# Two products of a feed-forward chunk in one 512-column matmul, with the halves added on VectorE

## The chip, the core and the metric

The kernel runs on one core of a Trainium2 chip. The metric is device time in microseconds of one execution, as a median over runs. The profile is of one such execution.

## The reference

The network works on one sequence of 256 tokens with 1024 channels, in float32. It has attention, recurrent and memory blocks, and six feed-forward blocks. The change touches only the latter:

```python
def squared_relu_mlp(h, w1, w2):          # twice, FF_DIM = 4096
    a = jax.nn.relu(h @ w1)
    return (a * a) @ w2

def swiglu(x, w_in, w_out):               # four times, D_FF = 2816
    gate, up = jnp.split(x @ w_in, 2, axis=-1)
    return (jax.nn.silu(gate) * up) @ w_out
```

## The kernel before

Weights stream from HBM in chunks of 1 MB (128x2048 float32), one after another through a ring of three slots. The queue SP loads a chunk into `raw`. ScalarE rounds it to fp32r in `w_hi` (`hi`, L628). VectorE subtracts, `raw - w_hi`, and has the rest in `w_lo` (`lo`, L1021). Activations are kept in the same two parts: `at_h` and `at_l` (or `mem_h` and `mem_l`), 8 k-tiles of 128 rows and 256 tokens, and `hid_h`, `hid_l` for the hidden layer. A product of two such pairs is three fp32r matmuls: high by high, high by low, low by high.

A column chunk (`col_chunk`, L1580) makes 256 hidden columns: two halves `i` of 128, in each 8 k-tiles `k`, in each the three products with 256 moving columns (the tokens), so 48 matmuls into one PSUM bank of `C`. In these chunks the weights are stationary. A row chunk (`row_chunk`, L1593) multiplies 256 hidden columns by their 1024 output columns in 24 matmuls of 512 columns, into the four banks of `Y`.

In a feed-forward block all engines follow an order written out by hand, in hardware loops (`Fori`):

- The squared-ReLU block (`relu_ff`) has 16 steps. TensorE does `up(j + 1)`, one column chunk, and then `down(j)`, the row chunk of the step before. Its hidden values come from ScalarE (`units`: Relu out of `C`, L753, Square into `full`, L755, Square into `hid_h`, L756) and VectorE (`units`: `hid_l`, L1155).
- The SwiGLU block (`swiglu`) has 11 steps. TensorE does the gate chunk and the up chunk of step `j + 1` (`gate_up`) and then `down(j)`. ScalarE takes the Silu of the gate chunk out of `C` (L788). VectorE multiplies it by the up chunk, twice (L1184 and L1185), and subtracts (L1187).
- The first chunks of a block (`front_part`, L1535) hold the activations stationary, so that work can start before the second block of tokens is normalised. Their result is transposed back (`front_turn`) into `C[:, 0, :]`.

Each instruction waits for its data on a semaphore: `chunk_done` counts finished chunks, `hid_lo` says that a step's hidden values are there, `lo_split` that a chunk's `w_lo` is. A load into a slot of `raw` waits for the `lo` of the chunk three before; a `hi` waits for the matmuls of the chunk three before. An engine takes its instructions in order, so what stands behind a wait waits too. Names such as `relu`, `full`, `pr` and `total` are parts of one buffer, which the profile calls arena.

Of the kernel before, what the change touches and what calls it, by code (L numbers as in the profile page):

```python
# [14 lines left out]
P = 128  # L15
# [26 lines left out]
class Counts:  # L42


    def __init__(self, norm, rms, xn, turned, x, y, chunk, copied, hid, hid_hi, up, head, ctx, rot, front):
        self.norm, self.rms, self.xn, self.turned, self.x, self.y = norm, rms, xn, turned, x, y
        self.chunk, self.copied = chunk, copied
        self.hid, self.hid_hi, self.up, self.head, self.ctx, self.rot, self.front = hid, hid_hi, up, head, ctx, rot, front

# [58 lines left out]
def build(nc, a, out):  # L108
# [15 lines left out]
    with ctx:  # L124
# [5 lines left out]
        xn = sb("xn", [P, TB, D])  # L130
        at_h = sb("at_h", [P, KT, S], f32r)
        at_l = sb("at_l", [P, KT, S], f32r)
        mem_h = sb("mem_h", [P, KT, S], f32r)
        mem_l = sb("mem_l", [P, KT, S], f32r)
        hid_h = sb("hid_h", [P, 3, 2 * S], f32r)
# [79 lines left out]
        full = pr  # L215


# [14 lines left out]
        first_gain_in = sem("first_gain_in")  # L232
        gains_in = [sem(f"gains_in{i}") for i in range(2)]
        front_ready, front_turned, front_hi = sem("front_ready"), sem("front_turned"), sem("front_hi")
        hid_hi = sem("hid_hi")
# [137 lines left out]
        def counts(s):  # L373

            if s[0] == "norm":
                return dict(norm=1, rms=s[1] != "same", xn=2, turned=4 * (s[1] != "out"))
            if s[0] == "post":
                return dict(norm=1, rms=1, x=2)
            if s[0] == "meanwhile":
                return dict(norm=2, rms=2, x=2, xn=2, turned=4, chunk=len(s[1]), copied=len(s[1]))  # L380
            if s[0] == "add":
                return dict(x=2)
            if s[0] == "cols":
                return dict(chunk=len(s[1]), copied=len(s[1]))
            if s[0] == "even_cols":
                return dict(norm=1, rms=1, xn=2, turned=4, chunk=len(s[1]), copied=len(s[1]))
            if s[0] == "rows":
                return dict(chunk=4, y=1)
            if s[0] == "relu_ff":
                return dict(chunk=2 * N_REL, y=1, copied=N_REL, hid=N_REL, hid_hi=N_REL, front=1)  # L390
            if s[0] == "swiglu":
                return dict(chunk=3 * N_GLU, y=1, copied=N_GLU, up=N_GLU - 1, hid=N_GLU, front=1)
# [12 lines left out]
        before, so_far = [], dict(norm=0, rms=0, xn=0, turned=0, x=0, y=0, chunk=0, copied=0, hid=0,  # L405
                                  hid_hi=0, up=0, head=0, ctx=0, rot=0, front=0)
        for s in net:
# [14 lines left out]
        def behind_post(at):  # L422

            return Counts(at.norm + 1, at.rms + 1, at.xn, at.turned, at.x + 2, at.y, at.chunk, at.copied, at.hid,
                          at.hid_hi, at.up, at.head, at.ctx, at.rot, at.front)

# [180 lines left out]
        def _(act):  # L607
# [132 lines left out]
            def front_out(at):  # L740

                act.wait_ge(front_turned, at.front + 1)
                return nc.scalar.activation(hid_h[:, 0, :], C[:, 0, :], ACT.Copy)

            def relu_ff(at, same):
                n = at.chunk

                def units(j, t=None):


                    step = (lambda v: v) if t is None else (lambda v: t * 3 + v)
                    act.wait_ge(chunk_done, n + 2 * j if t is None else t * 6 + (n + 2 * j))
                    nc.scalar.activation(relu[j % 3], C[:, j % 3, :], ACT.Relu).then_inc(cols_copied, 1)  # L753
                    act.wait_ge(cols_copied, step(at.copied + j + 1))
                    nc.scalar.activation(full[j % 3], relu[j % 3], ACT.Square)  # L755
                    nc.scalar.activation(hid_h[:, j % 3, :], relu[j % 3], ACT.Square).then_inc(hid_hi, 1)  # L756
# [15 lines left out]

                with nc.scalar.Fori(0, REL_TURNS) as t:
                    for j in range(1, 4):
                        two(j, t)
# [230 lines left out]
        def _(dve):  # L1006
# [137 lines left out]
            def front_out(at, turned_hi, count):  # L1144

                dve.wait_ge(turned_hi, count)
                V.tensor_tensor(hid_l[:, 0, :], C[:, 0, :], hid_h[:, 0, :].bitcast(f32), ALU.subtract).then_inc(hid_lo, 1)

            def relu_ff(at):
                n = at.chunk  # L1150

                def units(j, t=None):

                    dve.wait_ge(hid_hi, at.hid_hi + j + 1 if t is None else t * 3 + (at.hid_hi + j + 1))
                    V.tensor_tensor(hid_l[:, j % 3, :], full[j % 3], hid_h[:, j % 3, :].bitcast(f32),  # L1155
                                    ALU.subtract).then_inc(hid_lo, 1)
# [11 lines left out]

                with nc.vector.Fori(0, REL_TURNS) as t:
                    for j in range(1, 4):  # L1170
                        two(j, t)
# [344 lines left out]
        def _(pe):  # L1516
# [29 lines left out]
            def front_turn(at):  # L1546

                pe.wait_ge(front_ready, at.front + 1)
                for b in range(TB):
                    for k in range(2):  # L1550
                        last = nc.tensor.transpose(C[:, 0, k * S + b * P:k * S + (b + 1) * P],
                                                   full[0][:, b * S + k * P:b * S + (k + 1) * P], ident[:])
                last.then_inc(front_turned, 1)

            def col_chunk(n, kind, h, l, bank, t=None, split=None, some=range(2)):
# [103 lines left out]
            def relu_ff(at, same):  # L1659
                n = at.chunk  # L1660

                def up(j, t=None):

                    col_chunk(n + 2 * j - 1, "T", at_h, at_l, C[:, j % 3, :], t)

# [6 lines left out]
                front_one(n, front_bank(same), at, Y if same else C)  # L1672
                col_chunk(n + 1, "T", at_h, at_l, C[:, 1, :], some=[0])
                front_turn(at)
                col_chunk(n + 1, "T", at_h, at_l, C[:, 1, :], some=[1])
                down(0)
                with nc.tensor.Fori(0, REL_TURNS) as t:
                    for j in range(1, 4):
                        up(j + 1, t)
# [6 lines left out]
            def swiglu(at, same):  # L1686
                n = at.chunk
                h, l = (mem_h, mem_l) if same else (at_h, at_l)

                def gate_up(j, t=None):  # L1690
# [17 lines left out]
                front_part(n + 1, h, l, 1, Y[:, 1, :], split).then_inc(chunk_done, 1)  # L1708
                col_chunk(n + 2, "T", h, l, C[:, 2, :])
                front_turn(at)  # L1710
                col_chunk(n + 3, "T", h, l, C[:, 3, :])
                if at.rot > 0:
# [351 lines left out]
```

## Time and profile before

| | |
|---|---|
| median of 3 runs | 1869.29 us (1868.24 to 1869.43) |
| the profiled execution, its own time | 1868.2 us |
| its span, first to last instruction | 1866.2 us |
| mean granted TensorE clock | 0.995 of 2.4 GHz |
| busy: TensorE, VectorE, ScalarE | 97%, 55%, 46% of the span |

Between the end of the span and the time of the execution lie 2.0 us. The busy time of matmuls counts the overlap of one with the next, so the distance between the starts of neighbours is what one costs, not its own duration.

### The profile page before, as it was taken

Reading aid. Unit: us, or ns where it says so; the run is one execution under the profiler, and the core shown is the slowest. Engines: PE = TensorE matmul, PEld = TensorE weight load, DVE = VectorE, ACT = ScalarE, POOL = GpSimd, SP = SyncE. Lnnn points to the kernel's source line nnn. Section 1 sums busy time; section 2 is a strip of 40 time slices with the busy share of each in tenths; the row PEclk is TensorE's granted clock in tenths of the full one; section 3 lists DMA queues with packets and bytes.
Section 4 is the critical chain, followed back from the end, with each engine's and each line's share of the span. In section 5 each row is a group of like instructions: output and inputs, shape, how many; then the busy total and the mean of one; then the engine's idle time right before and its main releaser. Section 6 shows DMA issues by size and latency. Waiting matters only on the chain.

```text
span 1866.2 us, 29807 instructions
## 1 busy us (share of the span) xinstructions
PE 1814.5 (97%) x12635; PEld 1666.3 (89%) x12635; DVE 1020.6 (55%) x1037; ACT 857.0 (46%) x1044; POOL 71.0 (4%) x117
## 2 busy tenths in 40 slices
PE   7999999999999999999999999999999999899998
PEld 6989989998988989998999898899989998779997
DVE  5666465446566464446554554645565555765554
ACT  5535454446455454555333455533344334454333
POOL 1000000000120000000000011000000000110000
PEclk9999999999999999999999999999999999999999
DMA  8607446565546356554555544555555554336552
GB/s 270 218 23 226 136 159 189 193 189 180 175 153 203 112 169 194 190 190 162 189 180 181 169 129 149 178 181 185 191 168 195 187 180 158 113 114 204 180 181 89
DMA packets 224440, 318.69 MB, mean 171 GB/s; under 512 B 5569, under 2 KB 194129, under 8 KB 224353
## 3 DMA queue, kind: packets, MB, share of 16 engines
q1 hardware_dynamic: 219552, 301.48, 49.3%
q0 software_dynamic: 4800, 15.94, 2.7%
q8 instruction: 67, 1.10, 0.2%
q14 instruction: 21, 0.16, 0.0%
HBM read 316.35 MB, written 1.05 MB: 170 GB/s over the span
## 4 chain that ended last, share of the span: by engine, by line
PE 92%; DVE 4%; ACT 1%; DMA 1%; issue 1%; POOL 0%; SPq 0%; DVEq 0%; ACTq 0%
PE C L1580 45%; PE Y L1593 29%; PE Y L1580 7%; PE Y L1535 3%; DVE w_lo L1021 1%; DVE xn L1050 1%; DMA raw<-in_w_in_ab 1%; PE C L1982 1%; PE C L1829 1%; PE C L1737 1%; PE Y L1961 1%; PE C L1776 1%; PE Y L1784 1%; PE C L1638 1%; PE Y L1754 0%
## 5 line engine op out<-in xcount | busy, mean ns | idle before, releaser
L1021 DVE TENSOR_TENSOR w_lo<-raw,w_hi 128x2048 fp32r<-128x2048 f32 x284 | 650.2, 2290 | 486.0 <-ACT w_hi L628 485.7
L628 ACT ACTIVATE w_hi<-raw 128x2048 fp32r<-128x2048 f32 x284 | 542.4, 1910 | 361.0 <-PE Y L1593 219.8
L1580 PE MATMUL C<-at_h,w_hi 128*128 128x256 f32 x1664 | 465.2, 284 | 0.3 <-DVE at_l L1064 0.3
L1580 PE MATMUL C<-at_l,w_hi 128*128 128x256 f32 x1664 | 464.1, 283 | 0.7 <-DVE at_l L1064 0.7
L1580 PE MATMUL C<-at_h,w_lo 128*128 128x256 f32 x1664 | 464.0, 283 | 0.0
L1580 PEld LDWEIGHTS C<-at_l,w_hi 128*128 128x128 f32 x1664 | 316.2, 192 | 3.6 <-DVE at_l L1064 0.9
L1580 PEld LDWEIGHTS C<-at_h,w_hi 128*128 128x128 f32 x1664 | 316.1, 192 | 3.2 <-issue 1.0
L1580 PEld LDWEIGHTS C<-at_h,w_lo 128*128 128x128 f32 x1664 | 316.1, 192 | 0.0
L1593 PE MATMUL Y<-w_hi,hid_h 128*128 128x512 f32 x656 | 204.4, 393 | 3.5 <-issue 3.5
L1593 PE MATMUL Y<-w_lo,hid_h 128*128 128x512 f32 x656 | 203.0, 390 | 0.0
L1593 PE MATMUL Y<-w_hi,hid_l 128*128 128x512 f32 x656 | 202.7, 390 | 0.0
L1593 PEld LDWEIGHTS Y<-w_lo,hid_h 128*128 128x128 f32 x656 | 123.5, 188 | 26.6
L1593 PEld LDWEIGHTS Y<-w_hi,hid_l 128*128 128x128 f32 x656 | 123.4, 188 | 26.2
L1593 PEld LDWEIGHTS Y<-w_hi,hid_h 128*128 128x128 f32 x656 | 118.7, 189 | 24.4 <-issue 4.3
L1580 PE MATMUL C<-mem_h,w_hi 128*128 128x256 f32 x448 | 126.8, 283 | 0.0
L1580 PE MATMUL C<-mem_h,w_lo 128*128 128x256 f32 x448 | 126.8, 283 | 0.0
L1580 PE MATMUL C<-mem_l,w_hi 128*128 128x256 f32 x448 | 126.8, 283 | 0.0
L788 ACT ACTIVATE arena<-C 128x512 f32<-128x512 f32 x40 | 23.9, 597 | 153.0 <-PE C L1580 153.0
L1580 PEld LDWEIGHTS C<-mem_l,w_hi 128*128 128x128 f32 x448 | 86.0, 192 | 0.5
L1580 PEld LDWEIGHTS C<-mem_h,w_hi 128*128 128x128 f32 x448 | 86.0, 192 | 0.5
L1580 PEld LDWEIGHTS C<-mem_h,w_lo 128*128 128x128 f32 x448 | 86.0, 192 | 0.0
L1580 PE MATMUL Y<-at_h,w_hi 128*128 128x256 f32 x272 | 77.9, 286 | 0.0
(277 smaller groups left out, 2377.8 us busy)
## 6 DMA issues: line engine op xcount, KB each, us to landing
raw<-in_ffn_w_in SPq DMA_DIRECT2D x88, 1024.0 KB, 5.1
raw<-in_w_ff SPq DMA_DIRECT2D x64, 1024.0 KB, 5.3
raw<-in_ffn_w_out SPq DMA_DIRECT2D x44, 1024.0 KB, 4.9
raw<-in_w_mem_kv SPq DMA_DIRECT2D x16, 1024.0 KB, 5.3
raw<-in_w_qkv SPq DMA_DIRECT2D x12, 1024.0 KB, 5.1
raw<-in_sb_w_qkv SPq DMA_DIRECT2D x12, 1024.0 KB, 5.1
raw<-in_w_in_ab SPq DMA_DIRECT2D x10, 1024.0 KB, 8.0
raw<-in_w_mem_q SPq DMA_DIRECT2D x8, 1024.0 KB, 5.5
```

Source lines behind the costliest of these rows:

```text
L628: nc.scalar.activation(w_hi[:, n % RING, :], raw[:, n % RAW, :], ACT.Copy).then_inc(hi_split, 1)
L788: nc.scalar.activation(relu[j % 2], C[:, 2 * (j % 2), :], ACT.Silu).then_inc(cols_copied, 1)
L1021: V.tensor_tensor(w_lo[:, n % RING, :], raw[:, n % RAW, :], w_hi[:, n % RING, :].bitcast(f32), ALU.subtract).then_inc(lo_split, 1)
L1050: return V.scalar_tensor_tensor(xn[:, b, :], src, stat[:, 6, j:j + 1], gain[:, at.norm % 2, :], ALU.mult, ALU.mult)
L1535: last = mm(to[:, b * S:(b + 1) * S], still[:, k, part], moving[:, k, :], start=j == 0 and k == 0, stop=j == 2 and k == KT - 1)
L1580: last = mm(to, *passes[k][j], start=step == 0, stop=step == 3 * KT - 1)
L1593: last = mm(Y[:, 2 * b + half, :], still[:, part], moving[:, k, half * 512:(half + 1) * 512], start=first and k == 0 and j == 0, stop=end ...
L1638: last = nc.tensor.transpose(banks[:, 2 * b + h, k * P:(k + 1) * P], xn[:, b, (4 * h + k) * P:(4 * h + k + 1) * P], ident[:])
L1737: last = mm(C[:, i % 2, b * S:(b + 1) * S], qT[:, 2 * i + k, b * P:(b + 1) * P], mem_kT[:, 2 * i + k, :], start=k == 0, stop=k == 1)
L1776: last = nc.tensor.transpose(C[:, 2 + h % 2, k * P:(k + 1) * P], pair_pr[p % 3][:, h % 2, k * P:(k + 1) * P], ident[:])
L1784: last = mm(to[64 * (h % 2):64 * (h % 2) + 64, kb * P:S], vt[:, kb, value(h) * 64:value(h) * 64 + 64], head_pT[h % 4][:, kb * S:S + kb * P ...
L1829: mm(to[:, 0:SEEN], suffix_c, keep, start=False, stop=False, skip_group_check=True)
```

## The change

`at_h` and `at_l` become two halves of one tensor `at_hl` (and likewise `mem_hl`), so that for each k-tile the 256 high and the 256 low columns lie side by side. In the feed-forward loops `pair_chunk` takes the place of `col_chunk`. For each k-tile it issues one 512-column matmul, whose left half is `w_hi` by high and whose right half is `w_hi` by low, and one 256-column matmul, `w_lo` by high, which is added to the right half. A chunk then fills two banks of `C` in place of one, and the hidden columns are the sum of the two halves of each bank. VectorE makes this sum with `reduce_sum` over 128x1024 values in PSUM, into `total` in SBUF, whence ScalarE and VectorE go on. In `swiglu` the gate chunk now always has banks 0 and 1 and the up chunk banks 2 and 3, so TensorE waits for the sum of the step before (`gate_summed`, `up_summed`) ahead of writing them. `front_turn` goes to `Y[:, 2, :]`. The loops of `relu_ff` do six steps in a turn in place of three.

```diff
+        at_hl = sb("at_hl", [P, KT, 2, S], f32r)
+        mem_hl = sb("mem_hl", [P, KT, 2, S], f32r)
+        at_h, at_l, mem_h, mem_l = (t[:, :, i, :] for t in (at_hl, mem_hl) for i in range(2))
...
+        total = pT
...
+        def halves_of(pair):
+
+            return C[:, 2 * pair:2 * pair + 2, :].rearrange("p i (a n) -> p i n a", a=2)
...
@@ ScalarE, relu_ff units
-                    act.wait_ge(chunk_done, n + 2 * j if t is None else t * 6 + (n + 2 * j))
-                    nc.scalar.activation(relu[j % 3], C[:, j % 3, :], ACT.Relu).then_inc(cols_copied, 1)
+                    act.wait_ge(up_summed, step(at.summed + j))
+                    nc.scalar.activation(relu[j % 3], total[j % 3], ACT.Relu).then_inc(cols_copied, 1)
@@ ScalarE, swiglu gate
-                    act.wait_ge(chunk_done, step(6, n + 3 * j))
-                    nc.scalar.activation(relu[j % 2], C[:, 2 * (j % 2), :], ACT.Silu).then_inc(cols_copied, 1)
+                    act.wait_ge(gate_summed, step(2, at.up + j))
+                    nc.scalar.activation(relu[j % 2], total[0], ACT.Silu).then_inc(cols_copied, 1)
@@ VectorE, relu_ff units
+                    dve.wait_ge(chunk_done, n + 2 * j if t is None else t * 6 + (n + 2 * j))
+                    V.reduce_sum(tiles(total[j % 3], 2), halves_of(j % 2), X).then_inc(up_summed, 1)
                     dve.wait_ge(hid_hi, at.hid_hi + j + 1 if t is None else t * 3 + (at.hid_hi + j + 1))
@@ VectorE, swiglu units
                     dve.wait_ge(chunk_done, step(6, n + 3 * j + 1))
+                    V.reduce_sum(tiles(total[1], 2), halves_of(1), X).then_inc(up_summed, 1)
                     dve.wait_ge(cols_copied, step(2, at.copied + j + 1))
-                    up = C[:, 2 * (j % 2) + 1, :]
+                    dve.wait_ge(up_summed, step(2, at.summed + j))
+                    up = total[1]
@@ VectorE, swiglu
+                def gate(j, t=None):
+
+                    step = (lambda k, v: v) if t is None else (lambda k, v: t * k + v)
+                    dve.wait_ge(chunk_done, step(6, n + 3 * j))
+                    if j >= 2:
+                        dve.wait_ge(cols_copied, step(2, at.copied + j))
+                    V.reduce_sum(tiles(total[0], 2), halves_of(0), X).then_inc(gate_summed, 1)
+
                 def three(j, t=None):
                     b = n + 2 + 3 * j + AHEAD
                     lo(b, t)
+                    gate(j + 1, t)
@@ TensorE
-                        last = nc.tensor.transpose(C[:, 0, k * S + b * P:k * S + (b + 1) * P],
+                        last = nc.tensor.transpose(Y[:, 2, k * S + b * P:k * S + (b + 1) * P],
...
+            def pair_chunk(n, hl, pair, t=None, some=range(2)):
...
+                for i in some:
+                    part = slice(i * P, (i + 1) * P)
+                    to = C[:, 2 * pair + i, :]
+                    for k in range(KT):
+                        mm(tiles(to, 2), wh[:, k, part], hl[:, k, :, :], start=k == 0, stop=False)
+                        last = mm(to[:, S:2 * S], wl[:, k, part], hl[:, k, 0, :], start=False, stop=k == KT - 1)
...
@@ TensorE, relu_ff
-                    col_chunk(n + 2 * j - 1, "T", at_h, at_l, C[:, j % 3, :], t)
+                    pair_chunk(n + 2 * j - 1, at_hl, j % 2, t)
...
-                with nc.tensor.Fori(0, REL_TURNS) as t:
-                    for j in range(1, 4):
+                with nc.tensor.Fori(0, REL_TURNS, 2) as t:
+                    for j in range(1, 7):
@@ TensorE, swiglu
-                    col_chunk(n + 3 * j - 1, "T", h, l, C[:, 2 * (j % 2), :], t)
-                    col_chunk(n + 3 * j, "T", h, l, C[:, 2 * (j % 2) + 1, :], t)
+                    if j >= 2:
+                        pe.wait_ge(gate_summed, at.up + j - 1 if t is None else t * 2 + (at.up + j - 1))
+                    pair_chunk(n + 3 * j - 1, hl, 0, t)
+                    if j >= 2:
+                        pe.wait_ge(up_summed, at.summed + j - 1 if t is None else t * 2 + (at.summed + j - 1))
+                    pair_chunk(n + 3 * j, hl, 1, t)
```

What stands in order on two engines shows the change in the instructions. On TensorE, the first matmuls of the loop of the squared-ReLU block, before:

```order
L1677 ISA
L1580 MATMUL C<-at_h,w_hi 128x256
L1580 MATMUL C<-at_l,w_hi 128x256
L1580 MATMUL C<-at_h,w_lo 128x256
L1580 MATMUL C<-at_h,w_hi 128x256
L1580 MATMUL C<-at_l,w_hi 128x256
L1580 MATMUL C<-at_h,w_lo 128x256
```

The same place on TensorE after the change:

```order
L1708 ISA
L1581 MATMUL C<-at_hl,w_hi 128x512
L1582 MATMUL C<-at_hl,w_lo 128x256
L1581 MATMUL C<-at_hl,w_hi 128x512
L1582 MATMUL C<-at_hl,w_lo 128x256
L1581 MATMUL C<-at_hl,w_hi 128x512
```

Where there were three matmuls of 256 columns for a k-tile, there are one of 512 and one of 256, and these two lengths alternate.

On VectorE, one step of the loop of the SwiGLU block, before (rows of register arithmetic stand between the instructions):

```order
L1021 TENSOR_TENSOR w_lo<-raw,w_hi 128x2048
L1020 REGISTER_ALU
L1021 TENSOR_TENSOR w_lo<-raw,w_hi 128x2048
L1182 REGISTER_ALU
L1184 TENSOR_TENSOR arena<-C,arena 128x512
L1185 TENSOR_TENSOR hid_h<-C,arena 128x512
L1186 REGISTER_ALU
L1187 TENSOR_TENSOR hid_l<-arena,hid_h 128x512
L1020 REGISTER_ALU
L1021 TENSOR_TENSOR w_lo<-raw,w_hi 128x2048
```

The same step on VectorE after the change:

```order
L1025 TENSOR_TENSOR w_lo<-raw,w_hi 128x2048
L1210 TENSOR_REDUCE arena<-C 128x512
L1024 REGISTER_ALU
L1025 TENSOR_TENSOR w_lo<-raw,w_hi 128x2048
L1188 TENSOR_REDUCE arena<-C 128x512
L1189 REGISTER_ALU
L1190 REGISTER_ALU
L1192 TENSOR_TENSOR arena<-arena 128x512
L1193 TENSOR_TENSOR hid_h<-arena 128x512
L1194 REGISTER_ALU
L1195 TENSOR_TENSOR hid_l<-arena,hid_h 128x512
```

The sum of the gate chunk now stands between the first two `lo` of a step, and that of the up chunk ahead of the three elementwise operations, whose operands are all in SBUF.

## Rows read from the trace of the kernel before

**Rows 1.** The page: busy time by engine, and the chain that ended last by line.

```profile
PE 1814.5 (97%) x12635; PEld 1666.3 (89%) x12635; DVE 1020.6 (55%) x1037; ACT 857.0 (46%) x1044; POOL 71.0 (4%) x117
...
PE C L1580 45%; PE Y L1593 29%; PE Y L1580 7%; PE Y L1535 3%; DVE w_lo L1021 1%; DVE xn L1050 1%; DMA raw<-in_w_in_ab 1%; PE C L1982 1%; PE C L1829 1%; PE C L1737 1%; PE Y L1961 1%; PE C L1776 1%; PE Y L1784 1%; PE C L1638 1%; PE Y L1754 0%
```

**Rows 2.** Windows view: busy time by engine in most of a SwiGLU block.

```profile
895.63:1053.90 158.27, 158.27 (x1105) 148.47 (x1105) 80.20 (x55) 60.70 (x42) 0.00 (x0) 1.00 0.56 186
```

**Rows 3.** Chain in order of time (start us, us, what): last steps of two blocks.

```profile
429.69 5.47 PE Y L1593 x24
435.15 5.75 PE C L1580 x48
440.91 8.20 PE Y L1593 x36
...
1031.47 11.51 PE C L1580 x96
1042.98 10.92 PE Y L1593 x48
```

**Rows 4.** Timeline, TensorE and its weight loads (start us, us): row chunk to column chunk.

```profile
333.56 0.62 PE L1593 MATMUL Y<-w_hi,hid_l 128*128 128x512 f32 x2
334.01 0.28 PE L1580 MATMUL C<-at_h,w_hi 128*128 128x256 f32 x1
...
335.09 0.28 PE L1580 MATMUL C<-at_h,w_hi 128*128 128x256 f32 x1
...
333.79 0.19 PEld L1580 LDWEIGHTS C<-at_h,w_hi 128*128 128x128 f32 x1
```

**Rows 5.** Timeline, TensorE, 850 to 871 us: 512-column fp32r and bf16, 128-column transposes.

```profile
850.99 0.62 PE L1593 MATMUL Y<-w_hi,hid_l 128*128 128x512 f32 x2
...
856.43 0.62 PE L1593 MATMUL Y<-w_hi,hid_l 128*128 128x512 f32 x2
...
858.25 4.71 PE L1654 MATMUL C<-zeros 128*128 128x512 bf16 x21
...
870.46 1.03 PE L1638 MATMUL C<-ident,xn 128*128 128x128 f32 x8
```

**Rows 6.** Timeline, TensorE: the first 512-column matmuls behind 256-column ones.

```profile
328.55 0.63 PE L1593 MATMUL Y<-w_hi,hid_h 128*128 128x512 f32 x2
329.01 0.62 PE L1593 MATMUL Y<-w_lo,hid_h 128*128 128x512 f32 x2
329.48 0.62 PE L1593 MATMUL Y<-w_hi,hid_l 128*128 128x512 f32 x2
```

**Rows 7.** Groups of instructions by form, VectorE (count, busy us, mean ns, idle before).

```profile
L1137 DVE SCALAR_TENSOR_TENSOR x<-Y,x 128x1024 f32<-128x1024 f32 x12 | 14.7, 1225 | 27.4 <-PE Y L1593 27.4
L1235 DVE TENSOR_REDUCE arena<-C 128x2 f32<-128x512 f32 x8 | 5.5, 692 | 11.6 <-PE C L1737 11.6
L1389 DVE RECIPROCAL arena<-arena 128x512 f32<-128x512 f32 x1 | 3.3, 3345 | 0.0
```

**Rows 8.** Timeline, ScalarE and VectorE: the hidden values of a squared-ReLU block's last step.

```profile
440.95 0.60 ACT L753 ACTIVATE arena<-C 128x512 f32<-128x512 f32 x1 [3.78 <-PE C L1580]
...
442.76 0.69 DVE L1155 TENSOR_TENSOR hid_l<-arena,hid_h 128x512 fp32r<-128x512 f32 x1 [3.27 <-ACT hid_h L756]
```

**Rows 9.** Timeline, ScalarE and VectorE: the last step of a SwiGLU block.

```profile
1037.26 0.60 ACT L788 ACTIVATE arena<-C 128x512 f32<-128x512 f32 x1 [3.78 <-PE C L1580]
...
1039.69 2.29 DVE L1021 TENSOR_TENSOR w_lo<-raw,w_hi 128x2048 fp32r<-128x2048 f32 x1 [3.88 <-ACT w_hi L628]
1043.02 0.69 DVE L1184 TENSOR_TENSOR arena<-C,arena 128x512 f32<-128x512 f32 x1 [1.04 <-PE C L1580]
...
1044.34 0.69 DVE L1187 TENSOR_TENSOR hid_l<-arena,hid_h 128x512 fp32r<-128x512 f32 x1
```

**Rows 10.** Waits (us, times, longest), and page: a DMA issue (KB, us to landing).

```profile
ACT w_hi L628 <- DMA raw<-in_w_in_ab: 7.5, 1, 7.5
...
raw<-in_ffn_w_in SPq DMA_DIRECT2D x88, 1024.0 KB, 5.1
```

More of the change, by code:

```diff
@@ L42, with __init__ @@
 class Counts:
-    def __init__(self, norm, rms, xn, turned, x, y, chunk, copied, hid, hid_hi, up, head, ctx, rot, front):
+    def __init__(self, norm, rms, xn, turned, x, y, chunk, copied, hid, hid_hi, up, head, ctx, rot, front, summed):
         self.norm, self.rms, self.xn, self.turned, self.x, self.y = norm, rms, xn, turned, x, y
         self.chunk, self.copied = chunk, copied
-        self.hid, self.hid_hi, self.up, self.head, self.ctx, self.rot, self.front = hid, hid_hi, up, head, ctx, rot, front
+        self.hid, self.hid_hi, self.up, self.head, self.ctx, self.rot, self.front, self.summed = hid, hid_hi, up, head, ctx, rot, front, summed
 def constants():
@@ L130, in build @@
         xn = sb("xn", [P, TB, D])
[L131 to L134, printed above, removed]
+        at_hl = sb("at_hl", [P, KT, 2, S], f32r)
+        mem_hl = sb("mem_hl", [P, KT, 2, S], f32r)
+        at_h, at_l, mem_h, mem_l = (t[:, :, i, :] for t in (at_hl, mem_hl) for i in range(2))
         hid_h = sb("hid_h", [P, 3, 2 * S], f32r)
@@ L233, in build @@
         gains_in = [sem(f"gains_in{i}") for i in range(2)]
+        gate_summed, up_summed = sem("gate_summed"), sem("up_summed")
         front_ready, front_turned, front_hi = sem("front_ready"), sem("front_turned"), sem("front_hi")
@@ L389, in counts @@
             if s[0] == "relu_ff":
-                return dict(chunk=2 * N_REL, y=1, copied=N_REL, hid=N_REL, hid_hi=N_REL, front=1)
+                return dict(chunk=2 * N_REL, y=1, copied=N_REL, hid=N_REL, hid_hi=N_REL, front=1, summed=N_REL - 1)
             if s[0] == "swiglu":
-                return dict(chunk=3 * N_GLU, y=1, copied=N_GLU, up=N_GLU - 1, hid=N_GLU, front=1)
+                return dict(chunk=3 * N_GLU, y=1, copied=N_GLU, up=N_GLU - 1, hid=N_GLU, front=1, summed=N_GLU - 1)
             if s[0] == "softmax":
@@ L405, in build @@
         before, so_far = [], dict(norm=0, rms=0, xn=0, turned=0, x=0, y=0, chunk=0, copied=0, hid=0,
-                                  hid_hi=0, up=0, head=0, ctx=0, rot=0, front=0)
+                                  hid_hi=0, up=0, head=0, ctx=0, rot=0, front=0, summed=0)
         for s in net:
@@ L424, in behind_post @@
             return Counts(at.norm + 1, at.rms + 1, at.xn, at.turned, at.x + 2, at.y, at.chunk, at.copied, at.hid,
-                          at.hid_hi, at.up, at.head, at.ctx, at.rot, at.front)
+                          at.hid_hi, at.up, at.head, at.ctx, at.rot, at.front, at.summed)
         SEEN_BLOCKS = ((0, P), (P, SEEN))
@@ L742, in front_out @@
                 act.wait_ge(front_turned, at.front + 1)
-                return nc.scalar.activation(hid_h[:, 0, :], C[:, 0, :], ACT.Copy)
+                return nc.scalar.activation(hid_h[:, 0, :], Y[:, 2, :], ACT.Copy)
             def relu_ff(at, same):
@@ L771, in two @@
                     hi(n + 2 + 2 * j + AHEAD, t)
-                with nc.scalar.Fori(0, REL_TURNS) as t:
-                    for j in range(1, 4):
+                with nc.scalar.Fori(0, REL_TURNS, 2) as t:
+                    for j in range(1, 7):
                         two(j, t)
@@ L1146, in front_out @@
                 dve.wait_ge(turned_hi, count)
-                V.tensor_tensor(hid_l[:, 0, :], C[:, 0, :], hid_h[:, 0, :].bitcast(f32), ALU.subtract).then_inc(hid_lo, 1)
+                V.tensor_tensor(hid_l[:, 0, :], Y[:, 2, :], hid_h[:, 0, :].bitcast(f32), ALU.subtract).then_inc(hid_lo, 1)
             def relu_ff(at):
@@ L1167, in two @@
                     lo(n + 2 + 2 * j + AHEAD, t)
-                with nc.vector.Fori(0, REL_TURNS) as t:
-                    for j in range(1, 4):
+                with nc.vector.Fori(0, REL_TURNS, 2) as t:
+                    for j in range(1, 7):
                         two(j, t)
@@ L1550, in front_turn @@
                     for k in range(2):
-                        last = nc.tensor.transpose(C[:, 0, k * S + b * P:k * S + (b + 1) * P],
+                        last = nc.tensor.transpose(Y[:, 2, k * S + b * P:k * S + (b + 1) * P],
                                                    full[0][:, b * S + k * P:b * S + (k + 1) * P], ident[:])
                 last.then_inc(front_turned, 1)
+            def pair_chunk(n, hl, pair, t=None, some=range(2)):
+                split_ready(n, t)
+                wh, wl = (w[:, n % RING, :].rearrange("p (k c) -> p k c", k=KT) for w in (w_hi, w_lo))
+                for i in some:
[4 more added lines that the diff above has]
+                        last = mm(to[:, S:2 * S], wl[:, k, part], hl[:, k, 0, :], start=False, stop=k == KT - 1)
+                if 1 in some:
+                    last.then_inc(chunk_done, 1)
             def col_chunk(n, kind, h, l, bank, t=None, split=None, some=range(2)):
@@ L1672, in relu_ff @@
                 front_one(n, front_bank(same), at, Y if same else C)
-                col_chunk(n + 1, "T", at_h, at_l, C[:, 1, :], some=[0])
+                pair_chunk(n + 1, at_hl, 1, some=[0])
                 front_turn(at)
-                col_chunk(n + 1, "T", at_h, at_l, C[:, 1, :], some=[1])
+                pair_chunk(n + 1, at_hl, 1, some=[1])
                 down(0)
-                with nc.tensor.Fori(0, REL_TURNS) as t:
-                    for j in range(1, 4):
+                with nc.tensor.Fori(0, REL_TURNS, 2) as t:
+                    for j in range(1, 7):
                         up(j + 1, t)
@@ L1688, in swiglu @@
                 h, l = (mem_h, mem_l) if same else (at_h, at_l)
+                hl = mem_hl if same else at_hl
                 def gate_up(j, t=None):
-                    col_chunk(n + 3 * j - 1, "T", h, l, C[:, 2 * (j % 2), :], t)
-                    col_chunk(n + 3 * j, "T", h, l, C[:, 2 * (j % 2) + 1, :], t)
+                    if j >= 2:
[4 more added lines that the diff above has]
+                    pair_chunk(n + 3 * j, hl, 1, t)
                 def down(j, t=None, end=False):
@@ L1708, in swiglu @@
                 front_part(n + 1, h, l, 1, Y[:, 1, :], split).then_inc(chunk_done, 1)
-                col_chunk(n + 2, "T", h, l, C[:, 2, :])
+                pair_chunk(n + 2, hl, 0)
                 front_turn(at)
-                col_chunk(n + 3, "T", h, l, C[:, 3, :])
+                pair_chunk(n + 3, hl, 1)
                 if at.rot > 0:
```

## The prediction, made before the changed kernel was run

> **What bounds the kernel now.** I read the busy shares of the page first, then the chain that ended last, and then, since a share of busy time says nothing of a single stage, the chain in order of time and a window over one SwiGLU block. TensorE is busy 97% of the span and the next engine 55%, and 45% of the span lies on the chain as column chunks of line 1580 [rows 1]. In the window TensorE is busy 158.27 of 158.27 us and VectorE 80.20 [rows 2]. In the chain the chunks stand end to end: the row chunk at 429.69, the column chunk at 435.15 and the next row chunk at 440.91 leave no gap; neither do 1031.47 and 1042.98 [rows 3]. So in the feed-forward loops nothing but the rate at which TensorE starts matmuls sets the time, and whatever is added on VectorE is free until it makes TensorE wait.
>
> **What a matmul costs.** From the first 256-column matmul at 334.01 to the one at 335.09 there are nine starts, 1.08 / 9 = 120 ns each [rows 4]. For 512 columns, 24 starts lie between 850.99 and 856.43, 5.44 / 24 = 226.7 ns [rows 5]. The columns themselves stream in 256 / 2.4 = 106.7 ns and 512 / 2.4 = 213.3 ns at the granted clock of 1.00 in the window [rows 2]. Each matmul therefore carries 13.3 ns beyond its columns, and the same at both lengths. That is the term on which the forecast rests: one instruction less saves one such charge, while the number of streamed columns, 768 per k-tile, stays.
>
> **The change, part by part.**
>
> *Matmuls.* Per k-tile it was 3 x 120 = 360 ns and becomes 226.7 + 120 = 346.7 ns, so 13.3 ns less. Both lengths have been measured only among their own kind, save at the seams of chunks. There, a 256-column matmul follows a 512-column one without loss: the last pair of 512 starts at 333.56 and the 256 at 334.01, which is 225 ns each [rows 4]. The load of its weights starts at 333.79, with the matmul before it, so it has that matmul's stream as cover. The changed chunks are 15 for each of the two squared-ReLU blocks and 20 for each of the four SwiGLU blocks (the first chunk, or the first two, are made by the front part and stay). That is 30 + 80 = 110 chunks with 16 k-tiles each, 1760 in all. 1760 x 13.3 ns = 23.4 us.
>
> The bounds of this price: at worst the seam in the other direction recurs. The first 512-column matmuls behind 256-column ones start at 328.55, 329.01 and 329.48 in pairs, 0.93 / 4 = 232 ns each, and up to 235 in the second pair [rows 6]. Then a k-tile costs 235 + 120 = 355 and the change saves 5 x 1760 = 8.8 us. At best the 256-column matmul, with its load hidden behind a long one, falls toward the 128-column transposes' distance, (1.03 - 0.27) / 7 = 109 ns, where 0.27 is about what the last one's own duration adds [rows 5]. A k-tile is then 336 and the saving 24 x 1760 = 42 us. I take 13.3, since the charge is equal at two lengths and the seam loss fades within a few matmuls.
>
> The Trainium skill, on the page "TensorE: Matmul & The Clock Gate", section "Back-to-back issue gap", puts the distance of warm matmuls at N / 2.4 plus 2.5 ns. By that the merge would save 2.5 x 1760 = 4.4 us only. The trace has a row that agrees, the bf16 matmuls at 858.25 (21 in 4.71 us, so (4.71 - 0.40) / 20 = 216 ns), but the fp32r rows, which are those of this change, do not [rows 5].
>
> *Sums on VectorE.* 110 reductions of 1024 columns out of PSUM are added. The trace has none of this form. The nearest rows are a 1024-column operation out of PSUM at 1225 ns and a reduction over 512 columns at 692 ns [rows 7]; both say about 1.2 us. The lower bound is 0.69 us, if only the 512 results counted. The upper one, at the rate of the slowest row (3345 ns for 512), is 6.7 us. I take 1.23 us, as both nearer rows give one column per step. What hides them: per SwiGLU step VectorE has three `lo` of 2.29 us and 2.0 us of elementwise work [rows 9], 8.9 us, and with 2.5 us of sums 11.4, against a step of 16.98 us that shrinks to 16.55. In a squared-ReLU step it has 2 x 2.29 + 0.69 + 1.23 = 6.5 us, and stands about 1.8 us more in the wait for ScalarE, against 11.0 us.
>
> *The longer chain to the hidden values.* In the loops a row chunk comes a whole chunk or two after the column chunk it needs, and the chain is tight only at a block's end. In the squared-ReLU block the last column chunk ends at 440.91, the values are ready at 443.45 [rows 3, 8], and the second to last row chunk covers until 440.91 + 5.47 = 446.38. A sum of 1.23 us and a handshake of some 0.05 put them at 444.7, 1.6 us to spare. Behind the sum on VectorE wait `hid_l` and the next `lo`; it slides from 444.6 to 445.9, and the chunk it makes is of the following stage, more than 5 us later. In the SwiGLU block the Silu at 1037.26 slides by 1.3 us, with it the `hi` behind it and the `lo` that began at 1039.69, which ends at 1043.3 in place of 1041.98 [rows 9]. That is 0.3 us after the up chunk is done at 1042.98. The sum ends at 1044.5, and `hid_l` at about 1046.5, where the cover goes to 1048.45 [rows 3]. Again 1.9 us to spare, so I price it at nothing. With the cover gone each microsecond of delay costs one at six block ends.
>
> *Banks and loads.* The new waits of TensorE on `gate_summed` come after an up chunk and a row chunk, 11 us behind the gate chunk; the sum is there after 1.3. No load is late: in the whole trace ScalarE's `hi` waited once for a DMA, at the start [rows 10]. A `lo` that slides by 1.3 to 1.6 us moves its slot's load, which lands 5.1 us after issue [rows 10], while the slot is wanted only when the chunk after next is done, some 9 us or more behind that `lo`. ScalarE and VectorE reading `total` in SBUF in place of PSUM, the front's transpose into `Y`, and the longer loop body cost nothing that I can place: TensorE showed no gap at any turn of a loop [rows 3].
>
> **The sum.** 1868.2 - 23.4 = 1844.8 us for an execution such as the profiled one. The median of the runs lies 1.1 us above the profiled execution, so I expect 1845.9 as a median, say 1846.
>
> **The rivals.**
>
> *Alternating lengths keep the seam's loss.* For it speaks that the only 512-column matmuls seen right behind 256-column ones are slower (232 to 235 ns) [rows 6]. Against it: they lose as a group of six or so, also where they follow each other, and the change has equally many seams back. It gives 1868.2 - 8.8 = 1859.4, as a median 1860.5. Chance 0.12.
>
> *The charge is not per matmul.* If what a merge saves is only what the bf16 row shows beyond its columns, 216 - 213.3 = 2.7 ns, it is 4.8 us, and the median 1864.5. Against it stand the equal 13.3 ns at two lengths. The page's rule named above would give the same within 0.4 us. Chance 0.05.
>
> *More is saved,* as the load of a long matmul's weights or the pair's shared bank costs less than a charge each: up to 42 us, 1827. Chance 0.06.
>
> *The sum is slow, and VectorE becomes the bound.* The place is the SwiGLU step: 8.9 us plus two sums fill 16.98 us once a sum takes 4.0 us; from there on the kernel is slower, for the gain is gone and each further 0.1 us costs 36 x 0.2 = 7 us. At 6.7 us a sum, the step takes 22.3 us, 5.3 more in 36 steps, so 190 us more, some 2060 before the squared-ReLU blocks are counted. For it speaks only that the reduction reads two values 256 columns apart, a form no row shows. Against it, the reduction row [rows 7]. Chance 0.04.
>
> **How the numbers follow.** The forecast itself has 0.73; its own range, with the load and handshake terms a few microseconds off, is 1841 to 1852. The range of 8 in 10 takes in the seam rival: 1840 to 1861. A change of under 0.2% (3.7 us) can't be told from none here. Faster by more: 0.73 + 0.12 + 0.06, and nearly all of the 0.05, since 4.8 us is just over, so 0.94. Same: 0.02. Slower: 0.04.
>
> **What would show it.** In the changed profile the chain should have 32 matmuls of a column chunk in 16 x 346.7 = 5.55 us in place of 5.75 (x48), steps of 11.01 and 16.56 us, still without gaps; VectorE's reduction at about 1.23 us; the second to last and the last row chunk of each block still end to end. A start distance of 512-column matmuls in these chunks above 232 ns would be the seam rival; a wait of TensorE for `hid_l` or for a sum would prove my slack wrong; a reduction above 3 us would turn the sign into a question.

## The result, and the profile after

The changed kernel takes 1857.18 us as a median of 4 runs (1855.62 to 1857.87), against 1869.36 us before (1868.24 to 1870.82, 4 runs). The ratio is 0.9939, with a 95% interval of 0.9926 to 0.9952. It is faster, by 12.2 us, about half of the 23.4 us that were forecast. The profiled execution took 1857.76 us, its span is 1856.0 us.

The first rows are of the changed kernel's page: busy time by engine, the chain that ended last by line, and the costliest group of each of the new lines (the form, count, busy us, mean ns). The line numbers are those of the changed kernel: 1581 is the 512-column matmul of `pair_chunk`, 1582 the 256-column one, 1624 the row chunk, 1611 `col_chunk`.

```profile
PE 1806.5 (97%) x10875; PEld 1574.8 (85%) x10875; DVE 1151.2 (62%) x1147; ACT 859.4 (46%) x1044; POOL 71.0 (4%) x117
...
PE Y L1624 29%; PE C L1581 22%; PE C L1582 11%; PE C L1611 11%; PE Y L1611 7%; PE Y L1552 3%; DVE w_lo L1025 1%; DVE xn L1054 1%; PE C L2018 1%; DMA raw<-in_w_in_ab 1%; PE C L1865 1%; PE C L1773 1%; PE C L1812 1%; PE Y L1997 1%; PE C L1669 1%
...
L1581 PE MATMUL C<-at_hl,w_hi 128*128 128x512 f32 x1440 | 511.3, 399 | 0.0
L1582 PE MATMUL C<-at_hl,w_lo 128*128 128x256 f32 x1440 | 405.0, 281 | 0.0
...
L1210 DVE TENSOR_REDUCE arena<-C 128x512 f32<-128x1024 f32 x40 | 49.0, 1225 | 55.7 <-PE C L1582 55.7
```

The 45% of column chunks on the chain [rows 1] are now 22 + 11 + 11, the last of them in chunks that the change leaves alone. The sum of the gate chunk took 1225 ns, the other two 1218 and 1224, and VectorE's share rose from 55 to 62%. Both new matmul groups show no idle time before them. The windows view of a SwiGLU block, which answers to [rows 2], says so too: TensorE is busy all of it.

```profile
895.63:1048.00 152.37, 152.37 (x794) 129.79 (x794) 99.88 (x73) 58.46 (x38) 0.00 (x0) 1.00 0.56 189
```

So no wait has come in. The steps are nevertheless too long. In the chain in order of time (start us, us, what) the row chunks of neighbouring steps lie 11.11 us apart in a squared-ReLU block (5.640 for the column chunk and 5.467 for the row chunk) and 16.79 us in a SwiGLU block (11.290 and 5.504). Before it was 11.22 and 16.98 [rows 3]; 11.01 and 16.56 were forecast.

```profile
294.96 5.46 PE Y L1624 x24
306.06 5.46 PE Y L1624 x24
...
987.37 5.50 PE Y L1624 x24
1004.16 5.50 PE Y L1624 x24
```

Where the time goes is seen in the timeline of TensorE (start us, us):

```profile
948.68 0.40 PE L1581 MATMUL C<-at_hl,w_hi 128*128 128x512 f32 x1
948.91 0.28 PE L1582 MATMUL C<-at_hl,w_lo 128*128 128x256 f32 x1
949.02 0.40 PE L1581 MATMUL C<-at_hl,w_hi 128*128 128x512 f32 x1
949.26 0.28 PE L1582 MATMUL C<-at_hl,w_lo 128*128 128x256 f32 x1
949.38 0.40 PE L1581 MATMUL C<-at_hl,w_hi 128*128 128x512 f32 x1
949.62 0.28 PE L1582 MATMUL C<-at_hl,w_lo 128*128 128x256 f32 x1
949.74 0.40 PE L1581 MATMUL C<-at_hl,w_hi 128*128 128x512 f32 x1
```

From 948.68 to 949.74 there are three pairs in 1.06 us, 353.3 ns each, where 346.7 had been forecast and three matmuls of 256 columns took 360. The pattern repeats after three pairs: the long one is followed after 233, 241 and 236 ns, the short one after 117, 120 and 113.

For the comparisons below, one number was taken from every trace: the six feed-forward blocks, each from the first transpose of `front_turn` to the start of its last row-chunk matmul. It leaves out the rest of the network, which no kernel here changes and which differed by up to 6 us between executions (840.6 to 846.8 us). The sum is 1020.9 us before and 1010.3 us after, 10.5 us less.

### The profile page after: what moved, and what is told of

Read it like the earlier page. It is cut to its first block, busy times and chain, and to the rows that moved or that the text cites. A ratio compares the mean times of both kernels' runs of the same rounds, so it can differ in the third digit from the quotient of the medians.

```text
span 1856.0 us, 26531 instructions
## 1 busy us (share of the span) xinstructions
PE 1806.5 (97%) x10875; PEld 1574.8 (85%) x10875; DVE 1151.2 (62%) x1147; ACT 859.4 (46%) x1044; POOL 71.0 (4%) x117
## 4 chain that ended last, share of the span: by engine, by line
PE 93%; DVE 4%; ACT 2%; DMA 1%; issue 1%; POOL 0%; SPq 0%; DVEq 0%; ACTq 0%
PE Y L1624 29%; PE C L1581 22%; PE C L1582 11%; PE C L1611 11%; PE Y L1611 7%; PE Y L1552 3%; DVE w_lo L1025 1%; DVE xn L1054 1%; PE C L2018 1%; DMA raw<-in_w_in_ab 1%; PE C L1865 1%; PE C L1773 1%; PE C L1812 1%; PE Y L1997 1%; PE C L1669 1%
## 5 line engine op out<-in xcount | busy, mean ns | idle before, releaser
L1581 PE MATMUL C<-at_hl,w_hi 128*128 128x512 f32 x1440 | 511.3, 399 | 0.0
L1582 PE MATMUL C<-at_hl,w_lo 128*128 128x256 f32 x1440 | 405.0, 281 | 0.0
L1581 PEld LDWEIGHTS C<-at_hl,w_hi 128*128 128x128 f32 x1440 | 271.0, 188 | 65.6
L1582 PEld LDWEIGHTS C<-at_hl,w_lo 128*128 128x128 f32 x1440 | 272.5, 189 | 2.1
L1581 PE MATMUL C<-mem_hl,w_hi 128*128 128x512 f32 x320 | 113.5, 399 | 0.0
L1611 PE MATMUL Y<-at_hl,w_hi 128*128 128x256 f32 x544 | 99.3, 285 | 0.0
L1582 PE MATMUL C<-mem_hl,w_lo 128*128 128x256 f32 x320 | 90.0, 281 | 0.0
L1611 PEld LDWEIGHTS Y<-at_hl,w_hi 128*128 128x128 f32 x544 | 84.7, 192 | 0.5 <-ACT arena L710 0.3
L1210 DVE TENSOR_REDUCE arena<-C 128x512 f32<-128x1024 f32 x40 | 49.0, 1225 | 55.7 <-PE C L1582 55.7
L1624 PE MATMUL Y<-w_hi,at_hl 128*128 128x512 f32 x288 | 79.6, 393 | 1.8 <-DVE at_hl L1486 1.6
L1611 PE MATMUL C<-at_hl,w_hi 128*128 128x256 f32 x448 | 77.4, 286 | 1.0 <-DVE at_hl L1068 1.0
```

The lines of the kernel that those rows point to most:

```text
L1210: V.reduce_sum(tiles(total[0], 2), halves_of(0), X).then_inc(gate_summed, 1)
L1581: mm(tiles(to, 2), wh[:, k, part], hl[:, k, :, :], start=k == 0, stop=False)
L1582: last = mm(to[:, S:2 * S], wl[:, k, part], hl[:, k, 0, :], start=False, stop=k == KT - 1)
L1611: last = mm(to, *passes[k][j], start=step == 0, stop=step == 3 * KT - 1)
L1624: last = mm(Y[:, 2 * b + half, :], still[:, part], moving[:, k, half * 512:(half + 1) * 512], start=first and k == 0 and j == 0, stop=end ...
```

## The experiments

The theory was that 512-column fp32r matmuls are slow behind shorter ones, whatever else the core does. The rivals were that the sums on VectorE or their waits take the missing 11 us, and that it is the operands: writing twice to the same half of a bank, or the load of new weights.

**TensorE alone, fifteen streams.** A kernel in which TensorE runs 48 matmuls or pairs of each kind, with nothing on the other engines. For the alternating streams:

```diff
+ for i in range(n):
+     mm(C[:, 2, :], W(2 * i), H(i, 512), start=i == 0, stop=False)
+     mm(C[:, 2, 256:512], W(2 * i + 1), H(i, 256), start=False, stop=i == n - 1)
```

> This kernel leaves the network out: TensorE alone runs fifteen streams of 48 matmuls or pairs, one after another, each from a source line of its own, and the output is zeros. Read is the mean distance of starts in each stream. All theories: 256 columns alone 120 ns, 512 alone 227 ns. Theory of lengths (a change of length between neighbours costs time, whatever the operands): fp32r pairs of 512 and 256 cost 353 ns in all of the same bank, another bank and the same weights; two and two falls to about 350 per pair, eight and eight to 347 to 348; 384 columns alone 173.3 ns, so 346.7 for two. Theory of the shared bank (adding to the half that the matmul before has just written costs time): 353 ns in the same bank, 347 in the other bank, and grouping changes nothing. Theory of weight loads (the load of new fp32r weights doesn't fit behind 256 columns): with the same kind of load 353, in bf16 pairs the sum of the two single distances.

Distances, from the starts in the trace, once a stream repeats (per matmul, or per pair of a long and a short one):

| stream | measured | columns / 2.4 + 13.3 ns each |
|---|---|---|
| 256 alone; 384 alone; 512 alone | 120.0; 173.3; 226.7 ns | 120.0; 173.3; 226.7 |
| 512 and 256 in turn, same bank | 353.3 | 346.7 |
| the same, 256 into another bank | 353.3 | 346.7 |
| the same, both with the same weights | 353.3 | 346.7 |
| two of 512, two of 256 | 348.3 | 346.7 |
| eight of 512, eight of 256 | 349.2 | 346.7 |
| 384 and 256 in turn | 293.3 | 293.3 |
| 128 alone; 512 and 128 in turn | 111.7; 340.0 | 66.7; 293.3 |
| bf16: 256 alone; 512 alone; in turn | 109.2; 215.8; 325.0 | |
| 512 in fp32r, 256 in bf16, in turn | 358.3 | |

The rows of three of them in the timeline: two and two, 384 alone, and bf16 in turn.

```profile
92.80 8.52 PE L97 MATMUL C<-h,w 128*128 128x384 f32 x48
...
101.86 0.62 PE L102 MATMUL C<-h,w 128*128 128x512 f32 x2
102.32 0.40 PE L104 MATMUL C<-h,w 128*128 128x256 f32 x2
...
103.95 0.63 PE L102 MATMUL C<-h,w 128*128 128x512 f32 x2
...
167.19 0.38 PE L128 MATMUL C<-hb,wb 128*128 128x512 bf16 x1
167.41 0.27 PE L129 MATMUL C<-hb,wb 128*128 128x256 bf16 x1
167.51 0.38 PE L128 MATMUL C<-hb,wb 128*128 128x512 bf16 x1
```

48 matmuls of 384 columns take from 92.80 to the next stream at 101.16, 174 ns each (the first seven distances are longer, then it is 173.3). Two and two cost 103.95 - 101.86 = 2.09 us for six pairs, 348.3 ns. In bf16 a pair costs 0.32 us, the sum of its parts. The whole loss of the changed kernel, 6.7 ns a pair, is there with VectorE and ScalarE idle; it is not a matter of the bank. Equal weights change nothing either, but they are loaded again each time. The bf16 pairs lose nothing, as the theory of weight loads expected, so the load is not ruled out. And 384 with 256 has no loss, so it isn't any change of length.

**TensorE alone, lengths and groups.** Eighteen further streams.

> The network is left out again: TensorE alone runs eighteen streams of fp32r matmuls, and the output is zeros. If any change of length costs, the pairs 512 and 384, 512 and 320, 512 and 224, 512 and 192, 480 and 256, 448 and 256, 448 and 320, 384 and 192 all lie some 7 ns above the sum of their columns at 2.4 GHz plus 26.7. The first streams have 384 and 256 at no loss, so the theory that only a matmul longer than some length is slow behind a shorter one expects a loss for 512 and perhaps 480 and 448, and none for 384 and 192. Groups of 3, 4, 6 and 16: if the loss is 26 ns for the first six long ones behind short ones less 7 given back, a pair costs 346.7 + 20 / g, so 351.7 at 4, 350 at 6 and 347.9 at 16; but two and two was at 348.3 where this gives 356.7, so it may instead be flat near 349 and fall only beyond 8. Moving columns from another buffer for the short one: 353.3 as in the kernel, if addresses play no part.

| stream | measured | columns / 2.4 + 13.3 for each matmul | loss |
|---|---|---|---|
| 512 and 384 | 413.3 ns | 400.0 | 13.3 |
| 512 and 320 | 380.0 | 373.3 | 6.7 |
| 512 and 224 | 343.3 | 333.3 | 10.0 |
| 512 and 192 | 344.4 | 320.0 | 24.4 |
| 480 and 256 | 333.3 | 333.3 | 0 |
| 448 and 256; 448 and 320 | 320.0; 346.7 | 320.0; 346.7 | 0 |
| 384 and 192 | 290.0 | 266.7 | 23.3 |
| 512 and 256 from another buffer | 353.3 | 346.7 | 6.7 |
| groups of 3; 4; 6; 16 | 350.0; 350.8; 350.0; 347.9 | 346.7 | 3.3; 4.2; 3.3; 1.3 |
| 512, 256, 256 in turn | 466.7 | 466.7 | 0 |
| 512, 512, 256 in turn | 586.7 | 573.3 | 13.3 |
| 320; 448; 480 alone | 146.7; 202.7; 216.7 | 146.7; 200.0; 213.3 | 0; 2.7; 3.3 |

```profile
99.08 0.38 PE L96 MATMUL C<-h,w 128*128 128x480 f32 x1
...
99.75 0.38 PE L96 MATMUL C<-h,w 128*128 128x480 f32 x1
99.96 0.28 PE L97 MATMUL C<-h,w 128*128 128x256 f32 x1
...
100.41 0.38 PE L96 MATMUL C<-h,w 128*128 128x480 f32 x1
```

These are four pairs of 480 and 256 in 100.41 - 99.08 = 1.33 us. With a short one of 224 to 384 columns, the pair loses time only with the full 512, and 480 with 256 has no loss. Two things limit this reading. The column for comparison is not the sum of the two single streams everywhere: 480 and 448 alone cost 16.7 and 16.0 ns beyond their columns and not 13.3, so their pairs with 256 are even some 3 ns faster than that sum. And a long matmul behind a short one doesn't lose as such: with two short ones behind each long one (512, 256, 256) the three cost just their price.

The losses with 192 and 128 columns are probably another matter. The stream of 128 columns alone has a load of weights every 111.7 ns, where the columns stream in 53.3, and in the pairs with 128, 192 and 224 columns two loads stand 108 ns apart at the closest. So the load may be what is late behind so short a matmul; no run here separates the two. The expectation that groups of 3 and 4 would cost 353 and 352 was wrong; groups lose 1.7 ns a pair at two, 3.3 to 4.2 at three to six, 2.5 at eight and 1.3 at sixteen.

**480 columns in the network.** The same test inside the kernel; left out is the product of the high weights with the low activations of the last 32 tokens, in seven of eight k-tiles.

```diff
-                        mm(tiles(to, 2), wh[:, k, part], hl[:, k, :, :], start=k == 0, stop=False)
+                        cols = 512 if k == 0 else 480
+                        mm(to[:, 0:cols], wh[:, k, part], hl[:, k, :, :].rearrange("p a b -> p (a b)")[:, 0:cols],
+                           start=k == 0, stop=False)
```

> As after the change, with the long matmul cut from 512 to 480 columns in seven of eight k-tiles, 1540 in all; left out is the weight-high by activation-low product for the last 32 tokens. The stream of 480 and 256 measured alone has 333.3 ns for a pair, its columns plus 26.7, where 512 and 256 has 353.3. If only the 512-column matmul is slow behind a shorter one, the pairs lose 20 ns each, 13.3 of it the columns left out, and the time falls by 1540 x 20 ns = 31 us to 1826 us. If every alternation of lengths costs the 6.7 ns in the kernel, only the columns go: 20.5 us, 1837 us.

Measured: 1821.78 us (1821.42 to 1825.38), ratio 0.9759 (0.9742 to 0.9775). The feed-forward blocks sum to 979.0 us, 31.3 less than after the change, as the theory of the full 512 columns says (31), and not 20.5. The rest of the 35 us between the medians lies outside these blocks, where this execution had the shortest time of all, 840.6 us; whether by chance is not shown.

**Groups of eight.**

```diff
-                    for k in range(KT):
-                        mm(tiles(to, 2), wh[:, k, part], hl[:, k, :, :], start=k == 0, stop=False)
-                        last = mm(to[:, S:2 * S], wl[:, k, part], hl[:, k, 0, :], start=False, stop=k == KT - 1)
+                    for k0 in range(0, KT, 8):
+                        for k in range(k0, k0 + 8):
+                            mm(tiles(to, 2), wh[:, k, part], hl[:, k, :, :], start=k == 0, stop=False)
+                        for k in range(k0, k0 + 8):
+                            last = mm(to[:, S:2 * S], wl[:, k, part], hl[:, k, 0, :], start=False, stop=k == KT - 1)
```

> In each half of a chunk the eight 512-column matmuls come first and then the eight of 256 columns; all else is as after the change. Theory of lengths: one seam pair per half in place of eight, some 20 ns per pair of seams, so a chunk of 16 x 346.7 + 2 x 20 ns = 5.59 us in place of 5.64, and 1851 to 1853 us. Theory of the sums (the missing 11 us go to VectorE and its waits) and theory of the shared bank with its access patterns: no change, 1857 us.

Measured: 1847.11 us (1846.24 to 1849.94), ratio 0.9889 (0.9872 to 0.9905). The feed-forward blocks sum to 1001.5 us, 8.9 less than with the pairs in turn. The timeline shows one chunk's halves (start us, us, count at the end):

```profile
908.86 2.00 PE L1582 MATMUL C<-at_hl,w_hi 128*128 128x512 f32 x8
910.70 1.11 PE L1584 MATMUL C<-at_hl,w_lo 128*128 128x256 f32 x8
911.65 2.00 PE L1582 MATMUL C<-at_hl,w_hi 128*128 128x512 f32 x8
```

A half takes 911.65 - 908.86 = 2.79 us, so a pair 349 ns, as in the stream alone. More was gained than the 4 to 6 us expected. A chunk takes 5.56 to 5.57 us where 5.59 had been worked out. And in a SwiGLU step the row chunk behind it is faster too, 5.50 us after the change and 5.47 with groups of eight, as it was before the change; in a squared-ReLU step it takes 5.47 in all three. The theories of the sums and of the shared bank, which expected 1857 us, are out.

**Groups of two and of sixteen.** Two k-tiles at a time is the edit above with 2 in place of 8. The diff is of the other kernel, with all sixteen long matmuls of a chunk ahead of its sixteen short ones (over both halves).

```diff
+                for j in range(2):
+                    for i in some:
+                        ...
+                        for k in range(KT):
+                            if j == 0:
+                                mm(tiles(to, 2), wh[:, k, part], hl[:, k, :, :], start=k == 0, stop=False)
+                            else:
+                                last = mm(to[:, S:2 * S], wl[:, k, part], hl[:, k, 0, :], start=False, stop=k == KT - 1)
```

> Two and two k-tiles: the stream measured alone has 348.3 ns for a pair against 353.3 when they alternate, so 1760 x 5 ns = 8.8 us less than after the change, about 1848 us. If the loss were a fixed charge for each change of length, half of the alternation's 6.7 would be left, 3.3 ns, and the time 1851 us.

> In a whole chunk the sixteen 512-column matmuls come first, those of both halves, and then the sixteen of 256. One pair of seams per chunk in place of two: 20 ns less for each of 110 chunks, 2.2 us below the kernel with groups of eight measured beside it before, so 1845 us. Theory that the order plays no part: 1857 us.

Measured: groups of two 1847.81 us (1846.89 to 1848.61), ratio 0.9886 (0.9870 to 0.9902), feed-forward blocks 1000.0 us. That is what the stream alone had said, 1848, and not the 1851 of a fixed charge for each change of length. Sixteen: 1846.07 us (1844.67 to 1848.22), ratio 0.9882 (0.9866 to 0.9899), blocks 999.4 us, 2.1 less than with eight, as expected from one pair of seams less. The three grouped kernels can't be told apart by their times; each beats both the kernel before and the changed one.

**The long matmul split again.** Sums, banks and waits stay, but in seven of eight k-tiles there are three matmuls of 256.

```diff
-                        mm(tiles(to, 2), wh[:, k, part], hl[:, k, :, :], start=k == 0, stop=False)
+                        if k == 0:
+                            mm(tiles(to, 2), wh[:, k, part], hl[:, k, :, :], start=True, stop=False)
+                        else:
+                            mm(to[:, 0:S], wh[:, k, part], hl[:, k, 0, :], start=False, stop=False)
+                            mm(to[:, S:2 * S], wh[:, k, part], hl[:, k, 1, :], start=False, stop=False)
```

> The 512-column matmul is split again into two of 256 in seven of eight k-tiles; the side-by-side halves, the sums on VectorE, the banks and all waits stay. If the sums and waits are hidden, the chunk is back at about 5.75 us and the time at 1868 to 1869 us. If they cost TensorE something, it is above the kernel before by that, up to 1880 us.

Measured: 1867.28 us (1864.37 to 1869.04), ratio 0.9995 (0.9985 to 1.0004), the feed-forward blocks at 1019.1 us against 1020.9 before. The blocks are 1.8 us shorter, and 220 k-tiles stay merged, which at the 6.7 ns that a merge saves in the changed kernel is 1.5 us. So this is just the kernel before: the sums and the new waits cost TensorE nothing.

**Each sum twice.** The first time into a spare buffer. Shown is the sum of the up chunk; the other two are doubled in the same way.

```diff
+                    V.reduce_sum(tiles(spare, 2), halves_of(1), X)
                     V.reduce_sum(tiles(total[1], 2), halves_of(1), X).then_inc(up_summed, 1)
```

> Each sum on VectorE is done twice, the first time into a spare buffer, 110 x 1.23 us more work on VectorE. If the sums are hidden with the slack that was worked out (1.6 and 1.9 us at the ends of blocks), there is still room and the time stays at 1857 us. If the missing gain is a wait on VectorE, it grows by several microseconds up to 135.

Measured: 1860.21 us (1859.20 to 1861.41), ratio 0.9955 (0.9939 to 0.9972), 3.0 us above the changed kernel. The feed-forward blocks sum to 1013.5, 3.2 more, all in the SwiGLU blocks (0.8 us each); the squared-ReLU blocks stay at 169.38. The timelines show the last `hid_l` of a SwiGLU block and the start of the last row chunk, first after the change:

```profile
1040.72 0.69 DVE L1195 TENSOR_TENSOR hid_l<-arena,hid_h 128x512 fp32r<-128x512 f32 x1
...
1043.09 0.62 PE L1624 MATMUL Y<-w_hi,hid_h 128*128 128x512 f32 x2
```

With each sum twice, TensorE waits ahead of the last row chunk:

```profile
1042.91 0.69 DVE L1198 TENSOR_TENSOR hid_l<-arena,hid_h 128x512 fp32r<-128x512 f32 x1
...
1043.65 0.73 PE L1628 MATMUL Y<-w_hi,hid_h 128*128 128x512 f32 x2 [0.48 <-DVE hid_l L1198]
```

After the change `hid_l` ends at 1041.41 and the row chunk starts at 1043.09 without a wait. Of these 1.67 us a handshake takes 0.05 (with each sum twice, from the end of `hid_l` at 1043.60 to the start at 1043.65), so 1.6 us were to spare where 1.9 had been worked out. With each sum twice `hid_l` comes 2.26 us later, reckoned from the block's start, and the row chunk 0.65 us later (872 ns between two starts that are else 227 apart); 2.26 - 1.6 is just that. The block loses 0.79 us, because behind the wait the matmuls start 335, 235, 233 and 236 ns apart before they are back at 227. In the squared-ReLU block the last `hid_l` ends at 443.18 and its row chunk starts at 444.65, which leaves 1.4 us with the handshake where 1.6 had been worked out; 1.23 us more fit. The expectation that the time would not move at all forgot that a SwiGLU step's end takes both sums. A wait beyond the cover costs its own length and here 0.14 us more.

## Why the prediction was right and wrong

- **The bound was read rightly.** TensorE's rate of starts sets the feed-forward blocks [rows 2, 3], before and after, and nothing on VectorE or ScalarE became a bound.
- **The charge of 13.3 ns a matmul is right** for a stream of one length at 256 and 512 columns, and 320 and 384, which the trace of before did not have, gave it again (146.7 and 173.3 ns). It is no law of all lengths: 448 and 480 columns have 16.0 and 16.7 ns, and 128 has 58.3. So the equality at two lengths, on which the forecast leaned, was less of a rule than it looked.
- **The step that failed is that a k-tile "becomes 226.7 + 120 = 346.7 ns, so 13.3 ns less".** Each price was of a stream of its own kind. In alternation a pair costs 353.3. So the term was 6.7 ns x 1760 = 11.7 us where 13.3 x 1760 = 23.4 had been written. Of it 1.3 us are lost again in the row chunks of the SwiGLU steps, which take 5.504 us in place of 5.468 (0.036 us in some 36 steps). 11.7 - 1.3 = 10.4, and 10.5 were measured in the blocks. The other 1.7 of the 12.2 us lie outside the blocks, where single executions differ by up to 6 us.
- **The rival was on the page.** "Alternating lengths keep the seam's loss" had [rows 6] for it and gave 1860.5 against 1857.2 measured. Its sign, a distance of the 512-column matmuls above 232 ns, is there: 233, 241 and 236. I set it aside because the change has as many seams back; that gain was real (113 to 120 ns for the short one, 117 on average), but smaller than the loss. Its size was off too: 235 ns for each long one is right (236.2 on average), but the short one is 116.9 and not 120.
- **The rule of the Trainium skill** ("TensorE: Matmul & The Clock Gate", "Back-to-back issue gap") was tested by the streams: N / 2.4 plus 2.5 ns holds in bf16 (109.2 and 215.8 ns for 256 and 512), and in bf16 two lengths in turn simply add. The fp32r distances of 256 and 512 columns lie 10.8 ns above it, and the measurement decides.
- **The sums.** 1.22 to 1.23 us, as taken from the nearest rows [rows 7]. The hidden values of the squared-ReLU block's end were ready 4.0 us after the chunk, at 443.18 with a chunk end at 439.18; 3.8 had been worked out. The slack at the ends of blocks was 1.4 and 1.6 us, not 1.6 and 1.9, still enough for the term to be nothing.
- **The range** of 1840 to 1861 held the time only because the seam rival was taken into it; the forecast's own range, 1841 to 1852, did not. That the grouped kernels come to 1846 to 1848 us, where the forecast lay, is no success of it: they are other kernels, in which the pair costs 348 to 349 ns.

What stays open is the mechanism: why 512 fp32r columns behind a shorter matmul lose time and 480 don't, why one long and two short ones lose nothing, and two long and one short 13.3 ns. Whether the streaming of columns or the load of fp32r weights is what is late is not shown either. Where two lengths alternate one by one, the losses are multiples of 3.3 ns (all but 512 and 192), and the pattern of starts repeats, so it is no random contention; more is not shown.

## What to carry to other kernels

A price taken from a long stream of equal instructions isn't the price in another neighbourhood: look for the seams in the trace and price the new order by them, above all where they are the only rows that show it. When fp32r matmuls of 512 and 256 columns are mixed on a bound TensorE, put them in runs; here the order alone was worth 9 to 11 us in the blocks, nearly as much as the merge. Work added on an engine that is 55% busy is free as long as the chain to the bound engine's next need has room, and that room can be worked out from the timeline, here to 0.2 or 0.3 us, and tested by doubling the work.

## What the runs showed of the hardware that was not expected

- fp32r, 512 columns right behind 224 to 384 columns: 6.7 to 13.3 ns lost per pair; with 480, 448 or 384 beside 256, and with 448 beside 320, 0.
- After a run of 256-column fp32r matmuls, the first 512-column ones start 233, 236, 228, 233 and 231 ns apart, then 227; the first two short ones after a long run 113 and 119, then 120. The balance is 20 ns per pair of such seams.
- The charge beyond the columns in a stream of one length: in fp32r 13.3 ns at 256, 320, 384 and 512 columns, 16.0 at 448 and 16.7 at 480; in bf16 2.5 ns at 256 and 512. Taking fp32r and bf16 in turn (512 and 256 columns) costs 358.3 ns a pair, where the single streams sum to 335.9.
- fp32r matmuls of few columns don't get faster in proportion: 128 columns alone cost 111.7 ns, where 256 cost 120.0. Their loads of weights also start every 111.7 ns there, and 108 ns apart at the closest in the mixed streams.
- A run of 512-column fp32r matmuls that started after a wait of TensorE (the last row chunk, with each sum twice) had distances of 335, 235, 233 and 236 ns before it was back at 227.
